# A two-block transformer kernel on one core: new step table and token-tile projections in the second mixer

## The chip, the cores and the metric

One core of one Trainium2 chip runs the whole program. The metric is the device time of one execution in microseconds (us), the median over runs: 1990.09 us before (three runs, 1989.8 to 1990.51). A difference below 0.2% (4 us) can't be told from none.

## The reference, cut to what matters

256 tokens of width 1024 in float32 go through a first block of two layers (feed forward, attention mixer, feed forward) and a second block of two layers. The change touches only the mixer of the second block:

```python
z = rms_norm(x, ln_mix) @ w_in          # split into nsa q,k,v..., gla q,k,v,r,low, mem q, merge
o_nsa = nsa_attention(...)              # compressed + selected + window attention
o_gla = gated_linear_attention(...)     # rms_norm(o, norm_g) * silu(r)
o_mem = memory_attention(...)
gates = sigmoid(merge + b_merge)        # three of width 1024
merged = (gates[:, :, 0] * (o_nsa @ w_branch[0])
          + gates[:, :, 1] * (o_gla @ w_branch[1])
          + gates[:, :, 2] * (o_mem @ w_branch[2]))
x = x + merged @ w_out
```

## The kernel before, in words

**The stream of weights.** All weights of the projections arrive as 616 pieces of 128x1024 float32 (512 KB), in the order of use. SP (the DMA queue) loads a piece into `raw`, ACT rounds it into `hi` (L1270), POOL subtracts the two into `lo` (L542), in place of `raw`; in the mixers POOL does it in four quarters. There are 7 places for `raw`/`lo` and 5 for `hi`, so ACT can round piece c only after TensorE is done with piece c-5. TensorE multiplies each piece as hi·hi, hi·lo and lo·hi (L569, L570, L571): 12 matmuls of 512 columns for each piece, for two token tiles (m = 0 and 1) of 128 tokens. `round_piece` stands in ACT's program four pieces ahead of its use.

**The order of the mixer.** `mix2_work` is a table written by hand: behind each of the four pieces of a strip (512 columns of `w_in`) or of a branch projection ("rows") it lists the small steps to do there. `mix2_order` makes one list of it, and TensorE (PE), ACT and VectorE (DVE) each walk through that list in order and do their own part of every step, so a step's place in it is its place on all three engines. Waits between engines are semaphores; each engine runs strictly in its order. A "take" (PSUM to SBUF, by ACT or DVE) stands behind the fourth piece of each strip, ahead of that piece's steps.

**The steps.** `mem_unit` t (mu): scores of unit t, transposes of t-1 (L750), outputs of t-2. `nsa` 0 to 6: the compressed keys, a chain of small operations between PE and DVE. `nsa_unit` t (nu): t = 0 is the compressed attention (PE L1077, DVE L2211 to L2231, ACT L1610 between them); odd t makes the scores (PE L773) of two units; every t > 1 transposes unit t-1 (L750, which waits for DVE's normalised probabilities, L1858, and for bank `turned`, freed by DVE's copy L1866); even t from 4 on also makes outputs (L760). `gla` 2: log-sigmoid on ACT and two scans on DVE (L2082, L2084). `decay` hp,i: i = 0 and 1 subtract on DVE (L2112), then ACT makes Abs and Exp (L1591, L1592), i = 2 and 3 multiply on DVE (L2121, L2122). `gla_unit` hp,t (gu): masked scores (PE L982 and, for t = 2, two extra matmuls L972 into `turned`; DVE L2148), for t = 2 and 4 first an output (PE L997) into `turned`, copied by DVE (L2133). `gla` 3 to 5 are the norm of the gated linear attention: squares on ACT (L1529), variance on DVE (L1726), the product with silu(r) (L2090), the root, the scaling (L2093); `gla` 6 and 7 transpose (L1032).

**The end of the mixer.** The branch projections come in the order 2 (memory), 0 (nsa), 1 (gla), four pieces each. Branch 2 and branch 0 use PSUM banks 0 to 3, two for each token tile; branch 1 uses 4 to 7. The strip ahead (`gr`, r of the linear attention) leaves in banks 0 and 1 by Silu on ACT (L1564), and an `exp_and_ln()` (preload of a table) follows it. The three gates' Sigmoids (L1627) stand behind the first three pieces of branch 2. DVE's `branch(b, m)` (L2266) multiplies gate and projection once all four pieces of the branch are through, for both token tiles; PE starts branch 0 when `branch` has counted both tiles of branch 2. After branch 1, `merged` is transposed and multiplied by `w_out`.

Of the kernel before, what the change touches and what calls it, by code (L numbers as in the profile page):

```python
# [15 lines left out]
ALU = mybir.AluOpType  # L16
# [3 lines left out]
P = 128  # L20
# [92 lines left out]

ROWS2 = {2: 0, 0: 0, 1: 4}


def mix2_work():

    windows, prep, mem, memory_in, gla, nsa = (
        [(name, i) for i in range(9)] for name in ("windows", "prep", "mem", "memory_in", "gla", "nsa"))  # L120
    cmp = [("cmp", k // 4, k % 4) for k in range(8)]
    mu = [("mem_unit", t) for t in range(6)]
    gu = [[("gla_unit", hp, t) for t in range(5)] for hp in range(2)]
    decay = [[("decay", hp, i) for i in range(4)] for hp in range(2)]
# [85 lines left out]
def tiles(a):  # L210
# [4 lines left out]

    "hi", "lo", "used", "quarter",

# [334 lines left out]
def pe_program(M, V, sem):  # L552
# [33 lines left out]

    def rows_tile(c, m, kt, a_hi, a_lo, bank, start, stop):

        slot, slot_hi = c % RING, c % RING_HI
        for i in range(2):  # L590
            w = slice(i * 512, i * 512 + 512)
            t = product(psum[:, bank + 2 * m + i, :], a_hi[:, kt, m * P:m * P + P], a_lo[:, kt, m * P:m * P + P],
                        hi[:, slot_hi, w], lo[:, slot, w], start, stop)
        return t

    def rows(c, kt, a_hi, a_lo, bank, start, stop=False, second=None):

        pe.wait_ge(sem["lo"], c + 1)
        for m in range(MT):
            if m and second:  # L600
                pe.wait_ge(sem[second[0]], second[1])
            t = rows_tile(c, m, kt, a_hi, a_lo, bank, start, stop)
        t.then_inc(sem["used"], 1)

    def half_rows(c, m, kt, a_hi, a_lo, bank, stop):

        if m == 0:
            pe.wait_ge(sem["lo"], c + 1)
        t = rows_tile(c, m, kt, a_hi, a_lo, bank, False, stop)
        if m:  # L610
            t.then_inc(sem["used"], 1)
        elif stop:
            t.then_inc(sem["f"], 1)

    def last_rows(c, kts, a_hi, a_lo, bank, turn, ylo={}):

        for m in range(MT):
            for i, kt in enumerate(kts):
                if m and i == len(kts) - 1 and turn:
                    turn()  # L620
                if m == 0 and i in ylo:
                    pe.wait_ge(sem["ylo"], ylo[i])
                half_rows(c + i, m, kt, a_hi, a_lo, bank, i == len(kts) - 1)

# [65 lines left out]
    def feed_forward(c, strips, gated, n0, turn_next):  # L690
# [20 lines left out]
        def down(c, s):  # L711
            pe.wait_ge(sem["ylo"], s + 1)
            for i in range(kts):
                rows(c + i, (s - n0) % 2 * kts + i, y_hi, y_lo, 4, s == n0 and i == 0)

# [14 lines left out]
        order = [(strips - s) % 2 * kts + i for s in ((2, 1) if gated else (1,)) for i in range(kts)]  # L730
        last_rows(c, order, y_hi, y_lo, 4, turn_next, {kts: n0 + strips} if gated else {})
        return c + 4
# [52 lines left out]
    def mix1(layer, c0, turn_next):  # L785
# [64 lines left out]
        for step in mix1_order():  # L850
# [48 lines left out]
            elif what == "rows":  # L899
                i, kt = step[1:]  # L900
                if i == 0:
                    pe.wait_ge(sem["z4"], layer + 1)
                pe.wait_ge(sem["y1lo"], 7 * layer + Y1_EVENT[kt])
                rows(c0 + 24 + i, kt, y_hi, y_lo, 0, i == 0, second=("z5", layer + 1) if i == 0 else None)
            elif what == "half":
                m, i = step[1:]
                kt = OUT_ORDER[-4:][i]
                pe.wait_ge(sem["y1lo"], 7 * layer + Y1_EVENT[kt])
                half_rows(c0 + 24 + KD - 4 + i, m, kt, y_hi, y_lo, 0, i == 3)
            elif what == "turn":  # L910
                turn_next()
# [4 lines left out]
    def mix2(layer, c0, turn_next):  # L916
# [39 lines left out]
        def gla_score(hp, u):  # L956
# [7 lines left out]
            if u == 2:  # L964
                wait_free("turned")
                order = [(0, None)] + order + [(1, None)]
            for hh, i in order:
                half = slice(64 * hh, 64 * hh + 64)
                if i is None:
                    if hh:  # L970
# [137 lines left out]
        for step in mix2_order():  # L1108
# [82 lines left out]
            elif what == "rows":  # L1191
                b, i = step[1:]
                if b == 2 and i == 0:
# [8 lines left out]
                pe.wait_ge(sem["y2lo"], 10 * layer + Y2_EVENT[kt])  # L1202
                rows(piece[step], kt, y_hi, y_lo, ROWS2[b], i == 0, i == 3)
            elif what == "last_branch":
# [6 lines left out]
                enter(V.merged, (0, 1, 2, 3), "merged", 4 * layer, c,  # L1211
                      lambda cc, m, j: rows_tile(cc, m, j, h_hi, h_lo, 4, j == 0, False), lambda j: j // 2)
                pe.wait_ge(sem["xlo"], 8 * n["feats"])
                last_rows(c + 4, range(4, KD), h_hi, h_lo, 4, turn_next)
                c += KD
# [23 lines left out]
def act_program(M, V, sem, landed):  # L1239
# [246 lines left out]
    def mix2(layer, c0, rstd):  # L1486
# [52 lines left out]
        for step in mix2_order():  # L1539
# [13 lines left out]
            elif what == "take":  # L1553
# [6 lines left out]
                elif name == "gr":  # L1560
# [5 lines left out]
                    t.then_inc(sem["z_gr"], 1)  # L1566
                    exp_and_ln()
            elif what == "prep" and step[1] == 0:
# [52 lines left out]
            elif what == "gate":  # L1621
# [68 lines left out]
def dve_program(M, V, sem):  # L1690
# [297 lines left out]
    def mix2(layer, c0, rstd):  # L1988
# [78 lines left out]
        def gla_step(i):  # L2067
# [61 lines left out]
        def gla_unit(hp, t):  # L2129
            if t in (2, 4):  # L2130
                m = t // 2 - 1
                dve.wait_ge(sem["go"], nxt("go"))
                dve.tensor_copy(V.gqk[:, m, S * hp:S * hp + S], psum[:, TURNED, S:2 * S]).then_inc(sem["og"], 1)  # L2133
            if t < 4:

# [125 lines left out]
        def branch(b, m):  # L2261

            g = V.merge[:, m, b * D:b * D + D]
            dve.wait_ge(sem["sigmoid"], 6 * layer + 2 * (2, 0, 1).index(b) + m + 1)
            bank = ROWS2[b] + 2 * m
            t = dve.tensor_tensor(g, g, flat(psum[:, bank:bank + 2, :]), ALU.mult)  # L2266
# [11 lines left out]
        for step in mix2_order():  # L2278
# [304 lines left out]
```

## Time and profile before

| | us |
|---|---|
| median of the runs | 1990.09 |
| the profiled execution's own time | 1993.09 |
| its span, first to last instruction | 1991.4 |
| PE busy (98%) | 1960.1 |
| POOL busy (80%) | 1594.6 |
| ACT busy (52%) | 1045.1 |
| DVE busy (36%) | 719.2 |

PE is the engine that matters: each us in which it isn't idle, or in which it runs at the full clock, is a us of the whole. The second block's mixers lie at about 1022 to 1310 us (layer 0) and 1510 to 1800 us (layer 1); layer 1's is the pattern of layer 0's, and all rows in order of time below are of layer 1. In a row of the timeline, "[0.97 <-ACT kT L1399]" means that the engine was idle for 0.97 us ahead of it and what ended that. Neighbouring operations of one engine overlap a little, so a row's time and the distance to the next row differ.

### The profile page before, as it was taken

The numbers are of one execution on the slowest core, as the hardware profiler recorded it, in microseconds if no ns is written. First come the engines' busy times: TensorE is split into PE (matmuls) and PEld (weight loads), VectorE is DVE, ScalarE is ACT, GpSimd is POOL, SyncE is SP. The second block draws the span as 40 slices with busy tenths as digits, with TensorE's granted clock in tenths as the row PEclk, the third lists the DMA queues.
The fourth block names the chain that finished last, engine by engine and source line by source line (L and its number), as shares of the span: only waits on it lengthen the run. The fifth ranks groups of instructions, "written<-read, shape, count | busy, mean of one in ns | idle before, by whom it ended". The sixth has DMA issues, their size and how long they took to land.

```text
span 1991.4 us, 26549 instructions
## 1 busy us (share of the span) xinstructions
PE 1960.1 (98%) x9698; PEld 1583.5 (80%) x9698; DVE 719.2 (36%) x1686; ACT 1045.1 (52%) x1748; POOL 1594.6 (80%) x1160
## 2 busy tenths in 40 slices
PE   9999999999999999999999999999999999999999
PEld 7888777888888877788887877788888777778887
DVE  3534444000300454410045667521115576642111
ACT  6445666444644566644475444654446554555443
POOL 7888776988788887698879577888888867788886
PEclk9999999999999999999999999999999999999999
DMA  6665434555665543556564333456657433335553
GB/s 234 234 207 178 153 125 153 186 190 187 214 212 188 173 165 117 169 188 247 190 253 159 108 119 124 147 173 228 204 178 264 138 128 117 125 133 196 182 186 131
DMA packets 98204, 348.63 MB, mean 175 GB/s; under 512 B 13436, under 2 KB 14108, under 8 KB 97820
## 3 DMA queue, kind: packets, MB, share of 16 engines
q1 hardware_dynamic: 97372, 345.80, 51.3%
q8 instruction: 78, 1.28, 0.3%
q10 hardware_dynamic: 704, 1.14, 0.2%
q14 instruction: 50, 0.41, 0.1%
HBM read 345.85 MB, written 1.05 MB: 174 GB/s over the span
## 4 chain that ended last, share of the span: by engine, by line
PE 95%; DVE 2%; POOL 1%; issue 1%; ACT 1%; DMA 0%; SPq 0%; DVEq 0%; ACTq 0%
PE psum L569 28%; PE psum L571 28%; PE psum L570 27%; PE psum L707 2%; PE psum L750 1%; PE psum L637 1%; PE psum L760 1%; POOL lo L542 1%; PE psum L982 1%; PE psum L773 1%; PE psum L740 1%; PE psum L1136 0%; PE psum L837 0%; PE psum L796 0%; DVE big L2112 0%
## 5 line engine op out<-in xcount | busy, mean ns | idle before, releaser
L542 POOL TENSOR_TENSOR lo<-raw,hi 128x256 fp32r<-128x256 f32 (+1 forms) x1156 | 1594.4, 1403 | 382.6 <-ACT hi L1270 354.9
L1270 ACT ACTIVATE hi<-raw 128x1024 fp32r<-128x1024 f32 x616 | 647.6, 1059 | 512.2 <-PE psum L571 485.7
L569 PE MATMUL psum<-hi,h_hi 128*128 128x512 f32 x1632 | 654.0, 401 | 1.9 <-POOL lo L542 1.4
L571 PE MATMUL psum<-hi,h_lo 128*128 128x512 f32 x1632 | 639.6, 392 | 0.0
L570 PE MATMUL psum<-lo,h_hi 128*128 128x512 f32 x1632 | 638.8, 391 | 0.0
L569 PEld LDWEIGHTS psum<-hi,h_hi 128*128 128x128 f32 x1632 | 308.5, 189 | 72.5 <-POOL lo L542 5.3
L571 PEld LDWEIGHTS psum<-hi,h_lo 128*128 128x128 f32 x1632 | 307.9, 189 | 66.4
L570 PEld LDWEIGHTS psum<-lo,h_hi 128*128 128x128 f32 x1632 | 308.3, 189 | 60.3
L569 PE MATMUL psum<-hi,y_hi 128*128 128x512 f32 x832 | 334.9, 402 | 4.9 <-DVE big L2266 4.9
L1811 DVE SCALAR_TENSOR_TENSOR big<-psum,small,big 128x256 f32<-128x256 f32 (+1 forms) x120 | 61.1, 550 | 749.5 <-ACT big L1363 749.5
L571 PE MATMUL psum<-hi,y_lo 128*128 128x512 f32 x832 | 326.2, 392 | 0.0
L570 PE MATMUL psum<-lo,y_hi 128*128 128x512 f32 x832 | 325.4, 391 | 0.0
L569 PEld LDWEIGHTS psum<-hi,y_hi 128*128 128x128 f32 x832 | 156.9, 189 | 40.0 <-DVE big L2266 5.7
L571 PEld LDWEIGHTS psum<-hi,y_lo 128*128 128x128 f32 x832 | 157.0, 189 | 34.2
L570 PEld LDWEIGHTS psum<-lo,y_hi 128*128 128x128 f32 x832 | 157.4, 189 | 30.3
L1412 ACT ACTIVATE soft<-soft,small 128x128 f32<-128x128 f32 (+1 forms) x120 | 54.6, 456 | 131.7 <-DVE small L1847 104.5
L1363 ACT ACTIVATE big<-psum,small 128x256 f32<-128x256 f32 (+1 forms) x120 | 57.2, 528 | 84.0 <-PE psum L571 84.0
L1819 DVE TENSOR_TENSOR y_lo<-psum,y_hi 128x512 fp32r<-128x512 f32 (+1 forms) x60 | 49.4, 823 | 38.3 <-ACT y_hi L1372 38.3
L1745 DVE SCALAR_TENSOR_TENSOR h_lo<-psum,special,h_hi 128x128 fp32r<-128x128 f32 x160 | 44.1, 343 | 42.5 <-ACT h_hi L1287 42.5
L1287 ACT ACTIVATE h_hi<-psum,special 128x128 fp32r<-128x128 f32 x160 | 44.6, 380 | 23.2 <-PE psum L637 23.2
L1372 ACT ACTIVATE y_hi<-psum 128x512 fp32r<-128x512 f32 (+1 forms) x60 | 42.8, 714 | 13.1 <-PE psum L707 13.1
L1866 DVE COPY soft<-psum 128x384 f32<-128x384 f32 (+2 forms) x68 | 35.4, 520 | 27.5 <-PE psum L750 27.5
(264 smaller groups left out, 1363.5 us busy)
## 6 DMA issues: line engine op xcount, KB each, us to landing
raw<-in_stream SPq DMA_DIRECT2D x616, 512.0 KB, 3.3
big<-in_w SPq DMA_DIRECT2D x14, 512.0 KB, 7.6
big<-in_post SPq DMA_DIRECT2D x6, 512.0 KB, 5.8
special<-in_b_merge SPq DMA_DIRECT2D x2, 1536.0 KB, 8.0
memkv<-in_mem SPq DMA_DIRECT2D x2, 1024.0 KB, 5.8
big<-in_band SPq DMA_DIRECT2D x2, 768.0 KB, 4.8
x<-in_x SPq DMA_DIRECT2D x2, 512.0 KB, 5.3
special<-in_special SPq DMA_DIRECT2D x2, 512.0 KB, 4.4
```

The source lines that it names most:

```text
L542: t = pool.tensor_tensor(M.lo[:, slot, w], M.raw[:, slot, w], f32(M.hi[:, slot_hi, w]), ALU.subtract)
L569: pe.matmul(out, lhs_hi, rhs_hi, start=start, stop=False)
L570: pe.matmul(out, lhs_hi, rhs_lo, start=False, stop=False)
L571: return pe.matmul(out, lhs_lo, rhs_hi, start=False, stop=stop)
L1270: act.activation(M.hi[:, slot_hi, :], M.raw[:, slot, :], ACT.Copy).then_inc(sem["hi"], 1)
L1287: t = act.activation(out_hi[:, k, toks], psum[:, bank, i * P:i * P + P], ACT.Copy, scale=1.0 if gain is None else gain[:, k:k + 1])
L1363: t = act.activation(act_s[:, m, :], psum[:, bank + m, 0:width], ACT.Silu if gated else ACT.Relu, scale=V.scale[:, m:m + 1])
L1372: act.activation(flat(out), flat(psum[:, bank:bank + kts // 2, :]), ACT.Copy).then_inc(sem["yhi"], 1)
L1412: t = act.activation(out, prob[:, w], ACT.Exp, scale=-1.0, bias=mn[:, i:i + 1], accum_out=total[:, i:i + 1])
L1745: t = dve.scalar_tensor_tensor(out_lo[:, k, toks], psum[:, bank, i * P:i * P + P], gain[:, k:k + 1], f32(out_hi[:, k, toks]), ALU.mult, AL ...
L1811: t = dve.scalar_tensor_tensor(prod_s[:, m, :], psum[:, bank + m, col:col + width], V.scale[:, m:m + 1], act_s[:, m, :], ALU.mult, ALU.mult)
L1819: dve.tensor_tensor(flat(y_lo[:, kt, :]), flat(psum[:, bank:bank + kts // 2, :]), f32(flat(y_hi[:, kt, :])), ALU.subtract).then_inc(sem["y ...
```

## The change

It moves steps in the table, gives branch 2 and branch 0 their PSUM banks by token tile, splits waits by token tile, and removes one of ACT's table preloads.

```diff
-ROWS2 = {2: 0, 0: 0, 1: 4}
+ROWS2 = {2: (2, 0), 0: (2, 0), 1: (4, 6)}          # banks of token tile 0, of token tile 1
...
-        "gqk": ([mu[1], nsa[0]], [mu[2]], [mu[3], nsa[1]], [nsa[6], nsa[2]]),
+        "gqk": ([mu[1]], [nsa[0], mu[2]], [mu[3], nsa[1]], [nsa[6], nsa[2]]),
         "gv": ([mu[4], nsa[3]], [gla[0]], [mu[5], nsa[4]], [gla[1], nsa[5]]),
-        ("merge", 0): ([nu[0], gla[2]], [decay[0][0]], [nu[1], decay[0][1]], [decay[0][2]]),
-        ("merge", 1): ([nu[2], decay[0][3]], [nu[3]], [gu[0][0]], [nu[4]]),
-        ("merge", 2): ([gu[0][1]], [nu[5]], [gu[0][2]], [nu[6]]),
+        ("merge", 0): ([gla[2], nu[0]], [decay[0][0]], [nu[1], decay[0][1]], none),
+        ("merge", 1): ([nu[2], decay[0][2]], [nu[3]], [decay[0][3]], [nu[4]]),
+        ("merge", 2): ([gu[0][0]], [nu[5]], [gu[0][1]], [nu[6], gu[0][2]]),
...
-        ("rows", 2): ([nu[17], gu[1][4]], [nu[18]], [gla[3]], [gla[4]]),
-        ("rows", 0): ([gla[5]], [gla[6]], [gla[7]], none),
+        ("rows", 2): ([nu[17]], [nu[18], gu[1][4]], [gla[3], gla[4]], [gla[5]]),
+        ("rows", 0): (none, [gla[6]], [gla[7]], none),
...
     def rows(c, kt, a_hi, a_lo, banks, start, stop=False, second=lambda: None):
         pe.wait_ge(sem["lo"], c + 1)
         for m in range(MT):
+            if m:
+                second()
             t = rows_tile(c, m, kt, a_hi, a_lo, banks, start, stop)
+            if stop and m == 0:
+                t.then_inc(sem["rows"], 1)
...
             if u == 2:                                   # gla_score
-                wait_free("turned")
-                order = [(0, None)] + order + [(1, None)]
+                order = order[:4] + [(0, None)] + order[4:] + [(1, None)]   # the wait now at (0, None)
...
                 if b == 2 and i == 0:                    # PE, rows
-                    evicted(len(names) + 1)
                     evicted(len(names))
+                    second = lambda: evicted(len(names) + 1)
                 if b == 0 and i == 0:
-                    pe.wait_ge(sem["branch"], 4 * layer + 2)
+                    pe.wait_ge(sem["branch"], 4 * layer + 1)
+                    second = lambda: pe.wait_ge(sem["branch"], 4 * layer + 2)
...
                     t.then_inc(sem["z_gr"], 1)           # ACT, behind the Silus of "gr"
-                    exp_and_ln()
...
                     act.activation(w, w, ACT.Sigmoid).then_inc(sem["sigmoid"], 1)
-            elif what == "branch":
-                if step[1:] == (2, 0):
+                if b == 1:                               # behind the last gate
                     exp_and_ln()
...
+            elif i == 3:                                 # DVE, gla_step
+                dve.wait_ge(sem["og"], n["og"])
+                dve.wait_ge(sem["z_gr"], layer + 1)
+                own(dve.tensor_tensor(r3, r3, f3, ALU.mult))
             elif i == 4:
                 dve.wait_ge(sem["ss"], nxt("ss"))
                 variance(V.cells8, P)
-                dve.wait_ge(sem["z_gr"], layer + 1)
-                own(dve.tensor_tensor(r3, r3, f3, ALU.mult))
...
                 b, m = step[1:]                          # DVE, branch
-                dve.wait_ge(sem["used"], piece["rows", b, 3] + 1)
+                if m:
+                    dve.wait_ge(sem["used"], piece["rows", b, 3] + 1)
+                else:
+                    dve.wait_ge(sem["rows"], nxt("rows"))
                 branch(b, m)
```

## Rows read from the trace of the kernel before

**Rows 1.** Page, busy time of each engine (us, share, instructions).
```profile
PE 1960.1 (98%) x9698; PEld 1583.5 (80%) x9698; DVE 719.2 (36%) x1686; ACT 1045.1 (52%) x1748; POOL 1594.6 (80%) x1160
```
**Rows 2.** Who PE waited for in layer 1's mixer: total us, times, longest.
```profile
PE psum L750 <- DVE soft L1858: 3.0, 2, 2.9
PE psum L569 <- DVE big L2266: 2.4, 1, 2.4
PE psum L972 <- DVE big L2133: 1.2, 2, 0.6
```
**Rows 3.** Table by windows: us, busy (x count) of PE, PEld, DVE, ACT, POOL; clock; DMA.
```profile
1096.00:1100.00 4.00, 4.00 (x11) 3.10 (x11) 3.08 (x7) 0.00 (x0) 2.99 (x5) 0.57 0.00 0
1540.00:1620.00 80.00, 77.66 (x427) 59.89 (x426) 45.66 (x104) 40.45 (x95) 66.00 (x88) 1.00 0.40 132
1642.00:1646.00 4.00, 4.00 (x14) 3.13 (x13) 4.00 (x8) 0.75 (x3) 3.86 (x4) 0.57 0.00 0
```
**Rows 4.** Timeline of PE and DVE around nsa[0]: start, us, operation, idle before.
```profile
1584.52 1.05 PE L1043 MATMUL psum<-consts,extra 128*128 128x32 f32 x8 [1.25 <-DVE soft L1866]
1594.12 0.60 PE L750 MATMUL psum<-consts,soft 128*128 128x128 f32 x4
...
1585.61 0.29 DVE L2162 COPY extra<-psum 128x128 f32<-128x128 f32 x1
1588.07 0.64 DVE L2166 TENSOR_SCALAR extra<-extra 128x128 f32<-128x128 f32 x1
1589.43 0.48 DVE L2055 TENSOR_SCALAR_CACHE_REDUCE soft<-psum,small 128x256 f32<-128x256 f32 x1 [0.72 <-PE psum L939]
```
**Rows 5.** Timeline of PE and DVE in merge strips 0 and 1.
```profile
1641.72 0.55 PE L750 MATMUL psum<-consts,soft 128*128 128x128 f32 x3 [2.88 <-DVE soft L1858]
...
1622.38 0.49 DVE L2211 TENSOR_TENSOR extra<-psum,consts 128x128 f32<-128x128 f32 x2 [2.62 <-PE psum L1077]
1626.31 0.68 DVE L2082 SCALAR_TENSOR_TENSOR big<-big,extra 128x512 f32<-128x512 f32 x1
1627.02 1.76 DVE L2084 TENSOR_TENSOR_SCAN extra<-consts,big 128x256 f32<-128x256 f32 x2
1638.35 1.21 DVE L2122 TENSOR_TENSOR big<-big,kT 128x1024 f32<-128x1024 f32 x1
1640.13 1.53 DVE L1858 TENSOR_SCALAR soft<-soft,small,extra 128x128 f32<-128x128 f32 x2
```
**Rows 6.** Table by windows, POOL's `lo` alone: us, busy of PE, PEld, POOL; clock, DMA.
```profile
1637.40:1647.05 9.65, 2.64 (x5) 1.08 (x4) 9.43 (x8) 0.82 0.16 54
1647.10:1662.05 14.95, 5.48 (x14) 2.80 (x15) 14.27 (x20) 1.00 0.44 142
```
**Rows 7.** Timeline of DVE and PE around nu[6] and gu[0][2].
```profile
1668.96 1.41 DVE L2308 SCALAR_TENSOR_TENSOR big<-psum,small,special 128x512 f32<-128x512 f32 x2 [1.37 <-PE psum L571]
1670.62 0.55 DVE L1866 COPY soft<-psum 128x384 f32<-128x384 f32 x1
1671.28 1.46 DVE L1858 TENSOR_SCALAR soft<-soft,small,extra 128x128 f32<-128x128 f32 x2
...
1664.45 0.34 PE L972 MATMUL psum<-memkv,big 64*128 64x128 f32 x1 [0.61 <-DVE big L2133]
```
**Rows 8.** Groups by line on ACT, 1735 to 1755 us: busy, mean ns.
```profile
L1627 ACT ACTIVATE big<-big 128x1024 f32<-128x1024 f32 x6 | 6.0, 1046 | 0.0
```
**Rows 9.** Timeline of ACT, DVE, PE and POOL at the end of the mixer.
```profile
1737.13 1.28 ACT L1259 ACT_TABLE_LOAD   x1
1751.49 1.04 ACT L1270 ACTIVATE hi<-raw 128x1024 fp32r<-128x1024 f32 x1
...
1751.67 2.35 DVE L2266 TENSOR_TENSOR big<-big,psum 128x1024 f32<-128x1024 f32 x2 [4.80 <-PE psum L571]
...
1754.08 0.50 PE L569 MATMUL psum<-hi,y_hi 128*128 128x512 f32 x1 [2.44 <-DVE big L2266]
1785.26 0.50 PE L569 MATMUL psum<-hi,h_hi 128*128 128x512 f32 x1 [0.44 <-POOL lo L542]
```

More of the change, by code:

```diff
@@ L214 @@
 SEMAPHORES = (
-    "hi", "lo", "used", "quarter",
+    "hi", "lo", "used", "rows", "quarter",
     "x_in0", "x_in1", "ident", "const", "rot", "pre1", "pre2", "par", "mem_in", "masks", "angles", "stored", "w1_0", "w1_1",
@@ L585, in strip_piece, with rows_tile @@
         t.then_inc(sem["used"], 1)
-    def rows_tile(c, m, kt, a_hi, a_lo, bank, start, stop):
+    def rows_tile(c, m, kt, a_hi, a_lo, banks, start, stop):
         slot, slot_hi = c % RING, c % RING_HI
@@ L591, in rows_tile, with rows, half_rows @@
             w = slice(i * 512, i * 512 + 512)
-            t = product(psum[:, bank + 2 * m + i, :], a_hi[:, kt, m * P:m * P + P], a_lo[:, kt, m * P:m * P + P],
+            t = product(psum[:, banks[m] + i, :], a_hi[:, kt, m * P:m * P + P], a_lo[:, kt, m * P:m * P + P],
                         hi[:, slot_hi, w], lo[:, slot, w], start, stop)
         return t
-    def rows(c, kt, a_hi, a_lo, bank, start, stop=False, second=None):
+    def rows(c, kt, a_hi, a_lo, banks, start, stop=False, second=lambda: None):
         pe.wait_ge(sem["lo"], c + 1)
         for m in range(MT):
-            if m and second:
-                pe.wait_ge(sem[second[0]], second[1])
-            t = rows_tile(c, m, kt, a_hi, a_lo, bank, start, stop)
+            if m:
+                second()
+            t = rows_tile(c, m, kt, a_hi, a_lo, banks, start, stop)
+            if stop and m == 0:
+                t.then_inc(sem["rows"], 1)
         t.then_inc(sem["used"], 1)
-    def half_rows(c, m, kt, a_hi, a_lo, bank, stop):
+    def half_rows(c, m, kt, a_hi, a_lo, banks, stop):
         if m == 0:
             pe.wait_ge(sem["lo"], c + 1)
-        t = rows_tile(c, m, kt, a_hi, a_lo, bank, False, stop)
+        t = rows_tile(c, m, kt, a_hi, a_lo, banks, False, stop)
         if m:
@@ L613, in half_rows, with last_rows @@
             t.then_inc(sem["f"], 1)
-    def last_rows(c, kts, a_hi, a_lo, bank, turn, ylo={}):
+    def last_rows(c, kts, a_hi, a_lo, banks, turn, ylo={}):
         for m in range(MT):
@@ L622, in last_rows @@
                     pe.wait_ge(sem["ylo"], ylo[i])
-                half_rows(c + i, m, kt, a_hi, a_lo, bank, i == len(kts) - 1)
+                half_rows(c + i, m, kt, a_hi, a_lo, banks, i == len(kts) - 1)
     def turned_tile(src, m, pairs, banks, ready, until):
@@ L713, in down @@
             for i in range(kts):
-                rows(c + i, (s - n0) % 2 * kts + i, y_hi, y_lo, 4, s == n0 and i == 0)
+                rows(c + i, (s - n0) % 2 * kts + i, y_hi, y_lo, (4, 6), s == n0 and i == 0)
         c += 4
@@ L730, in feed_forward @@
         order = [(strips - s) % 2 * kts + i for s in ((2, 1) if gated else (1,)) for i in range(kts)]
-        last_rows(c, order, y_hi, y_lo, 4, turn_next, {kts: n0 + strips} if gated else {})
+        last_rows(c, order, y_hi, y_lo, (4, 6), turn_next, {kts: n0 + strips} if gated else {})
         return c + 4
@@ L903, in mix1 @@
                 pe.wait_ge(sem["y1lo"], 7 * layer + Y1_EVENT[kt])
-                rows(c0 + 24 + i, kt, y_hi, y_lo, 0, i == 0, second=("z5", layer + 1) if i == 0 else None)
+                rows(c0 + 24 + i, kt, y_hi, y_lo, (0, 2), i == 0, second=lambda: pe.wait_ge(sem["z5"], layer + 1))
             elif what == "half":
@@ L908, in mix1 @@
                 pe.wait_ge(sem["y1lo"], 7 * layer + Y1_EVENT[kt])
-                half_rows(c0 + 24 + KD - 4 + i, m, kt, y_hi, y_lo, 0, i == 3)
+                half_rows(c0 + 24 + KD - 4 + i, m, kt, y_hi, y_lo, (0, 2), i == 3)
             elif what == "turn":
@@ L969, in gla_score @@
                 if i is None:
-                    if hh:
+                    if not hh:
+                        wait_free("turned")
+                    else:
                         pe.wait_ge(sem["rowtile"], nxt("rowtile"))
@@ L1192, in mix2 @@
                 b, i = step[1:]
+                second = lambda: None
                 if b == 2 and i == 0:
-                    evicted(len(names) + 1)
                     evicted(len(names))
+                    second = lambda: evicted(len(names) + 1)
                 if b == 0 and i == 0:
-                    pe.wait_ge(sem["branch"], 4 * layer + 2)
+                    pe.wait_ge(sem["branch"], 4 * layer + 1)
+                    second = lambda: pe.wait_ge(sem["branch"], 4 * layer + 2)
                 if b == 1 and i == 0:
@@ L1202, in mix2 @@
                 pe.wait_ge(sem["y2lo"], 10 * layer + Y2_EVENT[kt])
-                rows(piece[step], kt, y_hi, y_lo, ROWS2[b], i == 0, i == 3)
+                rows(piece[step], kt, y_hi, y_lo, ROWS2[b], i == 0, i == 3, second)
             elif what == "last_branch":
@@ L1211, in mix2 @@
                 enter(V.merged, (0, 1, 2, 3), "merged", 4 * layer, c,
-                      lambda cc, m, j: rows_tile(cc, m, j, h_hi, h_lo, 4, j == 0, False), lambda j: j // 2)
+                      lambda cc, m, j: rows_tile(cc, m, j, h_hi, h_lo, (4, 6), j == 0, False), lambda j: j // 2)
                 pe.wait_ge(sem["xlo"], 8 * n["feats"])
-                last_rows(c + 4, range(4, KD), h_hi, h_lo, 4, turn_next)
+                last_rows(c + 4, range(4, KD), h_hi, h_lo, (4, 6), turn_next)
                 c += KD
@@ L2133, in gla_unit @@
                 dve.tensor_copy(V.gqk[:, m, S * hp:S * hp + S], psum[:, TURNED, S:2 * S]).then_inc(sem["og"], 1)
+                n["og"] += 1
             if t < 4:
@@ L2264, in branch @@
             dve.wait_ge(sem["sigmoid"], 6 * layer + 2 * (2, 0, 1).index(b) + m + 1)
-            bank = ROWS2[b] + 2 * m
+            bank = ROWS2[b][m]
             t = dve.tensor_tensor(g, g, flat(psum[:, bank:bank + 2, :]), ALU.mult)
@@ L2336, in mix2 @@
                 b, m = step[1:]
-                dve.wait_ge(sem["used"], piece["rows", b, 3] + 1)
+                if m:
+                    dve.wait_ge(sem["used"], piece["rows", b, 3] + 1)
+                else:
+                    dve.wait_ge(sem["rows"], nxt("rows"))
                 branch(b, m)
```

## The prediction, made before the changed kernel ran

> **What bounds the kernel now.** I read the page's table of busy times first: PE is busy for 1960.1 of 1991.4 us [rows 1], so the whole is PE's work plus some 31 us in which it is idle or starts late. PE's matmuls stay as many and as large. The change can therefore only act through PE's idle time inside the two second-block mixers, and through what that idle time does to the clock. The second view was PE's list of waits over layer 1's mixer: 3.0 us for the probabilities (two waits, the longest 2.9), 2.4 for DVE's branch product, 1.2 for bank `turned` behind `gla_unit` [rows 2], and 1.25 ahead of nsa[0] [rows 4]. Layer 0 has the same waits to 0.1 us. The third view was the table by windows: in the 4 us behind the longest wait the granted clock is 0.57, that is, most of them ran at 1.2 GHz instead of 2.4. At 0.57, 4 x 0.43 = 1.7 us of PE time are lost. The 1.25 us wait has such a stretch behind it in layer 0 (1096 to 1100 us, 0.57) but not in layer 1 (clock 1.00 over 1540 to 1620 us) [rows 3]. So a wait over 2 us costs itself and 1.7 us more, one of 1.25 us sometimes does. The sums below are in us for one layer, on the profiled execution (1993.1 us, span 1991.4), and doubled at the end.
>
> **1. nsa[0] one piece later.** PE's 1.25 wait goes [rows 4]: the copy it waited for has a whole piece (2.7 us) to end. What is late next is DVE. Its nsa[0] chain of five operations (first at 1585.61, last ends at 1588.71: 3.1 us) ran beside a piece; now it stands ahead of mu[2]'s minimum, which started at 1589.43. PE would reach nsa[0]'s matmuls at about 1586.0 and end them at 1586.9; the chain then ends at 1590.1, 0.65 later than the minimum started before, and the probabilities behind it are ready at about 1593.4. PE arrives at their transpose (L750, 1594.12 before) 1.25 earlier, at 1592.9, and waits some 0.6. Net gain 0.6 (bounds 0 and 1.25). In layer 0 the low clock behind the old wait should go too: 1.7, once.
>
> **2. The probabilities of nsa unit 2's transpose.** PE waited 2.88 at 1641.72 for L1858, which ended at 1641.66 [rows 5]. Two things leave DVE's queue ahead of it. The linear attention's rest (L2082 0.68 and the scans, 2.5 together) ran behind nu[0]; now it goes ahead of it, into DVE's 2.62 of idle time before L2211. It waits for ACT's three operations there, which I put at 1618.8 to 1620.8, so it ends at 1623.4 and nu[0] starts 1.0 later: 1.5 of 2.5 is saved. And the first decay multiplication (L2121 and L2122, alike, 1.21 each with overlap, 2.3 together) moves behind that L1858. Together 3.8: ready at 1637.9, against PE's arrival at 1641.72 - 2.88 = 1638.8, or 1638.7 without the smaller wait of 0.17 of the same group [rows 2]. The cover is 0.8. I take the whole 2.88 + 0.17 + 1.7 for the clock = 4.75. Bounds: 2.05 (1 us of wait comes back and the clock falls all the same) and 4.75. What is late next: the last decay multiplication, needed at gu[0][0], which now stands one piece later; by the same count DVE ends it near 1646, PE comes near 1649.
>
> **3. gu[0][2] right behind nu[6].** Before, a piece lay between. Now PE transposes (L750), and its next matmul writes the same bank, so it waits for DVE's copy L1866, which stands behind the take of merge strip 2: L2308 starts when the piece ends (1668.96), L1866 ends at 1671.17, and PE is through with L750 at about 1670.05. A wait of 1.1. Then DVE still has L1858 (1.46, to 1672.74) ahead of the copy L2133 that frees the bank again. PE's output matmuls end near 1672.0, four of the scores (0.07 each) hide 0.3, and it waits some 0.9 more. New waits 2.0, against 0.61 before [rows 7]: a loss of 1.4. Behind PE are the scores of that unit and piece 0 of merge strip 3; nobody else is late for them. Bounds: a loss of 0.5 (L1858 takes about 0.7 where POOL is idle) and of 3.1 (the clock falls as well). For the clock I charge one fall over both layers.
>
> **4. Four scores ahead of the wait in `gla_score`.** For gu[1][2] the wait of 0.61 [rows 2] loses the time of four matmuls: gain 0.3 (0 to 0.6).
>
> **5. The end of the mixer.** The table load behind Silu goes (1.28), and `gr`'s and branch 2's banks no longer tie PE to ACT; PE wasn't waiting there. The load of Sigmoid's table stays, since it follows Silu's directly, and the load for Exp and Ln moves ahead of the squares. ACT's line from Silu's end at 1737.13 is full in both versions: three roundings, six Sigmoids of 1.0 [rows 8], two loads, a high part, the squares of 2.35, which ended before 1751.49 [rows 9]. By the same durations it comes to 1751.3. DVE now takes the variance of these squares *before* `branch(2, 0)`, so the branch product, free to start at 1749.3 by the new semaphore, starts at about 1751.45 (before: 1751.67). PE, which saves the 0.74 wait and gets here at 1750.7, needs only the first of the two products (2.35 / 2): it starts branch 0 near 1752.8 instead of 1754.08, still after 2 us of idle and so with the low clock. Gain 1.2. The second product ends at 1754.0, under PE's six matmuls at either clock. Behind it POOL is the next to be late: PE already waited 0.44 for `lo` at 1785.26 [rows 9], and pieces there come back to back. I keep 1.0. Bounds: 0.4, and 4.1 if wait and clock both go. L2090 (1.8) moves from the branch to a place where DVE was idle; nothing hangs on it.
>
> The rest (DVE's `branch(0, 0)` half a piece earlier, `z_gr` for one tile only) lies beside PE's work: nothing.
>
> **Sum.** 0.6 + 4.75 - 1.4 + 0.3 + 1.0 = 5.25 in each layer, 10.5 for two; plus 1.7 for layer 0's clock in step 1, less 1.7 for one fall in step 3: 10.5. The profiled execution would take 1982.6, and the median 1990.1 - 10.5 = **1979.6 us**.
>
> **A rule that speaks against it.** POOL's pieces took 9.43 / 2 = 4.7 us over 1637 to 1647, beside DVE's multiplications, and 14.27 / 5 = 2.9 over 1647 to 1662 [rows 6]. The Trainium skill (SBUF — State Buffer, section "SBUF: two separate sides") says that a DVE operation with two SBUF inputs and a GpSimd operation exclude each other for a whole instruction; the trace agrees as far as these numbers go. It would make a denser DVE queue a slower POOL, which is the last rival below.
>
> **Rivals.**
> - *Half of it comes back (0.18).* Step 2's cover of 0.8 is less than one operation, and step 3's two waits may both lower the clock. Then step 2 gives 2.9 (1 us of wait back in both layers, the low clock in one: 3.75 and 2.05) and step 3 costs 3.1: 0.6 + 2.9 - 3.1 + 0.3 + 1.0 = 1.7, with layer 0's 1.7 a gain of 5.1: 1985.0. For it: L1858 took 1.46 and 1.53 in two places. Against: each of these needs two waits to be longer than I count.
> - *The end's wait goes whole (0.12).* If ACT is 1.5 us earlier at the squares than I add up, PE meets no wait over 1 us and no low clock: 3.1 more in each layer, 1973.4. For it: the product itself could start at 1749.3. Against: ACT's line has no gap to lose.
> - *The waits are only exchanged (0.08).* DVE is the late engine from 1622 to 1647 without a pause; if the postponed multiplications make PE wait at gu[0][0] as long as it waited before, step 2 gives nothing: 0.5 in each layer and 1.7, 1987.4 or up to no change.
> - *POOL takes over, and it is slower (0.06).* Place: merge strips 0 to 3, 16 pieces, where PE takes about 4.0 a piece with the steps between. If the denser DVE keeps POOL at 4.7 for all of them, POOL falls behind by 0.7 x 16 = 11 less the 5 us of lead it has there, 6 us of waits, and with every such wait the clock (two falls, 3.4): 9.4 - 5.25 = 4 lost in each layer, about 1997. It decides once POOL's mean piece there passes 4.3; it was 3.5 (24.6 us for seven) in [rows 6].
>
> **How the numbers follow.** Forecast 0.56, 1979.6. Its own range is 1976 to 1983. For 8 in 10, I reach to the first rival above and partly to the second below: 1975 to 1986.5. A measurement of this kernel tells about 0.2%, 4 us, from no change. Faster by more: 0.56 + 0.12 + 0.15 of the first rival = 0.83. Within: 0.03 + 0.08 = 0.11. Slower: 0.06.
>
> **What would show it.** Step 1: no wait of L1043, one of about 0.6 at an L750 some 9 us later, clock 1.00 near 1096. Step 2: no wait over 1 us for L1858, clock 1.00 around 1640. Step 3: two new waits in nu[6] and gu[0][2], for L1866 and L2133, 1.1 and 0.9. Step 5: a wait of some 2 us for L2266 remains, DVE's product starts right behind the variance, and each of the two mixers has one table load less. Wrong would be: a wait for `lo` that grows past 2 us in a layer, the L1858 wait still there, or a gain below 5 us in all.

## The result and the profile after

The changed kernel takes **1975.14 us** (median of 4 runs, 1974.72 to 1976.92), the kernel before 1990.3 beside it (1989.8 to 1991.71): a ratio of 0.9918 [0.9907, 0.993]. It is faster, by more than forecast: 1979.6 was predicted, with 1976 to 1983 as the forecast's own range, so the time lies 0.9 below its lower end. The profiled execution took 1974.96 us (span 1972.9), against 1993.09 (1991.4): 18.5 us of span to explain, where the steps had given 10.5.

Page of the changed kernel: span, then busy times as in [rows 1].
```profile
span 1972.9 us, 26543 instructions
PE 1951.8 (99%) x9698; PEld 1578.3 (80%) x9698; DVE 719.3 (36%) x1686; ACT 1041.4 (53%) x1746; POOL 1592.1 (81%) x1160
```
PE has the same 9698 matmuls in 8.3 us less of busy time, though none was removed: most of that is the clock (four falls fewer, below, at 1.7 each: 6.8). The other 10 us are idle time that is gone. ACT has two instructions less, one table load in each of the two mixers.

Who PE waited for in layer 1's mixer of the changed kernel, as in [rows 2]: total us, times, longest.
```profile
PE psum L569 <- DVE big L2272: 2.0, 1, 2.0
PE psum L1000 <- DVE soft L1869: 1.2, 1, 1.2
PE psum L742 <- ACT kT L1404: 1.0, 1, 1.0
PE psum L569 <- POOL lo L542: 0.7, 2, 0.4
```
(The changed kernel has new line numbers, and in the kernels of the experiments they differ by one more or less: L2272 is the branch product that was L2266, L1869 the copy L1866, L1861 the probabilities L1858, L2138 the copy L2133; L752, L1000 and L975 were L750, L997 and L972.) The 2.9 for the probabilities, the two of 0.6 for L2133 and the 1.25 ahead of nsa[0] [rows 2, 4] are gone. L742's 1.0 was there before. One wait is new: 1.2 at L1000.

Table by windows of the changed kernel, as in [rows 3]: one of the times at which the clock had fallen before, nearly all of the time from layer 0's mixer to the branch wait of layer 1 (1040 to 1735), and the 4 us at that wait.
```profile
1096.00:1100.00 4.00, 4.00 (x27) 3.59 (x27) 3.56 (x10) 0.75 (x3) 2.01 (x3) 1.00 0.38 131
1040.00:1735.00 695.00, 684.86 (x3691) 545.64 (x3689) 347.85 (x834) 369.02 (x684) 559.28 (x568) 1.00 0.46 162
1735.00:1739.00 4.00, 3.35 (x8) 2.68 (x9) 3.86 (x7) 1.37 (x4) 3.67 (x6) 0.59 0.31 118
```
Before, the clock fell five times in the two mixers (behind both L1858 waits, both branch waits and one of the two 1.25 waits). Now it falls once, behind the branch wait of layer 1.

Timeline of the changed kernel around nsa[0], as in [rows 4].
```profile
1575.05 0.97 PE L1046 MATMUL psum<-consts,extra 128*128 128x32 f32 x8
1581.80 0.66 PE L752 MATMUL psum<-consts,soft 128*128 128x128 f32 x4
...
1576.06 0.29 DVE L2168 COPY extra<-psum 128x128 f32<-128x128 f32 x1 [1.28 <-PE psum L1046]
1578.14 0.23 DVE L2172 TENSOR_SCALAR extra<-extra 128x128 f32<-128x128 f32 x1
1578.40 0.48 DVE L2058 TENSOR_SCALAR_CACHE_REDUCE soft<-psum,small 128x256 f32<-128x256 f32 x1
...
1572.59 5.11 POOL L542 TENSOR_TENSOR lo<-raw,hi 128x256 fp32r<-128x256 f32 x7
1581.32 2.79 POOL L542 TENSOR_TENSOR lo<-raw,hi 128x256 fp32r<-128x256 f32 x4 [3.62 <-ACT hi L1275]
```
DVE's chain of five took 2.3 us (1576.06 to 1578.37), not the 3.1 of [rows 4], and PE went through L752 without a wait. POOL was idle from 1577.70: its next piece wasn't rounded yet. The last two operations of the chain, which started after that, took 0.29 and 0.23; beside POOL's piece they had taken 0.73 and 0.64.

Timeline of the changed kernel around gu[0][2], as in [rows 7].
```profile
1651.26 0.68 PE L1000 MATMUL psum<-big 128*128 128x128 f32 x4 [1.17 <-DVE soft L1869]
1651.87 0.72 PE L985 MATMUL psum<-memkv,big 64*128 64x128 f32 x8
1652.46 0.37 PE L975 MATMUL psum<-memkv,big 64*128 64x128 f32 x1
...
1651.22 0.67 DVE L1861 TENSOR_SCALAR soft<-soft,small,extra 128x128 f32<-128x128 f32 x2
1651.97 0.42 DVE L2138 COPY big<-psum 128x256 f32<-128x256 f32 x1
```
The wait of 1.1 for the copy is there as forecast (1.17). The second, of 0.9 for L2138, is not: L1861 took 0.67 us instead of 1.46, although POOL was at work beside it (one row of `lo`, 1646.36 to 1655.43), and the four scores ahead of the wait (eight matmuls of the trace, 1651.87 to 1652.46) cover the copy that ends at 1652.39.

Timeline of the changed kernel at the end of the mixer, as in [rows 9].
```profile
1730.42 1.28 ACT L1264 ACT_TABLE_LOAD   x1
1734.07 1.04 ACT L1275 ACTIVATE hi<-raw 128x1024 fp32r<-128x1024 f32 x1
...
1734.27 0.17 DVE L1729 TENSOR_SCALAR small<-small 128x8 f32<-128x8 f32 x1 [3.86 <-ACT big L1534]
1734.38 2.35 DVE L2272 TENSOR_TENSOR big<-big,psum 128x1024 f32<-128x1024 f32 x2
...
1735.65 0.73 PE L569 MATMUL psum<-hi,y_hi 128*128 128x512 f32 x1 [2.01 <-DVE big L2272]
```
This is step 5 as written: the product starts right behind the variance, PE after the first half of it, still after 2 us of idle.

**Stage by stage** (profiled executions, differences of the starts of the same PE instructions): the span ahead of the first mixer gave 1.0 us, which is no edit's (the start of one and the same PE instruction there lies between 1037.5 and 1039.1 us in the profiles of all kernels); layer 0's mixer 9.7; layer 1's 7.7; the end 0.1.

### The profile page after: what moved, and what is told of

Same layout as the page of the kernel before. It is cut to its first block, busy times and chain, and to the rows that moved or that the text cites. A ratio compares the mean times of both kernels' runs of the same rounds, so it can differ in the third digit from the quotient of the medians.

```text
span 1972.9 us, 26543 instructions
## 1 busy us (share of the span) xinstructions
PE 1951.8 (99%) x9698; PEld 1578.3 (80%) x9698; DVE 719.3 (36%) x1686; ACT 1041.4 (53%) x1746; POOL 1592.1 (81%) x1160
## 4 chain that ended last, share of the span: by engine, by line
PE 94%; POOL 2%; ACT 2%; DVE 1%; issue 0%; DMA 0%; SPq 0%; POOLq 0%; ACTq 0%; DVEq 0%
PE psum L569 28%; PE psum L571 27%; PE psum L570 27%; POOL lo L542 2%; PE psum L709 2%; PE psum L752 1%; PE psum L639 1%; PE psum L775 1%; PE psum L762 1%; PE psum L985 1%; PE psum L742 1%; ACT big L1631 1%; ACT hi L1275 0%; PE psum L1139 0%; PE psum L798 0%; PE psum L839 0%
## 5 line engine op out<-in xcount | busy, mean ns | idle before, releaser
L1869 DVE COPY soft<-psum 128x384 f32<-128x384 f32 (+2 forms) x68 | 35.4, 520 | 24.9 <-PE psum L752 24.9
```

## The experiments

Each kernel ran four or five times (the one of 5: 11 times) beside the kernel before, which took 1992.3 to 1993.1 us (medians of 9, 9, 15 and 9 runs) in these four sessions; the changed kernel, run again in two of them, took 1975.4 and 1975.71. Differences below are from 1975.5. The part ahead of the mixers, which no edit touches, varied by 1.6 us between the profiles, so a difference of 1 or 2 us between two medians carries little. "A fall" is a short stretch in which TensorE's granted clock drops from 2.4 to 1.2 GHz, as behind the waits of [rows 3]; PE loses 1.7 us in it. Experiments are called by their numbers.

**1. The middle alone** (the kernel before with the table's new rows for merge strips 0 to 2).
```diff
-        ("merge", 0): ([nu[0], gla[2]], [decay[0][0]], [nu[1], decay[0][1]], [decay[0][2]]),
+        ("merge", 0): ([gla[2], nu[0]], [decay[0][0]], [nu[1], decay[0][1]], none),
...                                                   # and the rows of strips 1 and 2
```


> The kernel before with the new merge rows of the table alone (linear attention's rest ahead of nu[0], decay multiplications later, gu[0][2] right behind nu[6]). Theory A, waits as the trace of the changed kernel has them and 1.7 us for each stretch of low clock: the L1858 wait goes with its clock (4.75 in each layer), gu[0][2] costs one wait of 1.17, nothing for the second: 3.6 in each layer, 1983. Theory B, the sizes of my forecast (two new waits, 1.4, and one fall of the clock): 2.5 in each layer, 1985.3.

1984.31 us (1982.52 to 1985.34), ratio 0.9959 [0.9946, 0.9971].
Its waits in layer 1:
```profile
PE psum L569 <- DVE big L2266: 2.4, 1, 2.4
PE psum L997 <- DVE soft L1866: 1.9, 2, 1.2
PE psum L569 <- POOL lo L542: 1.4, 2, 1.2
PE psum L1043 <- DVE soft L1866: 1.3, 1, 1.3
PE psum L972 <- DVE big L2133: 1.2, 2, 0.6
```
The L1858 wait and the clock fall behind it are gone in both layers; of the 2.0 us of new waits that I had added for gu[0][2], 1.2 came (L997), and the 0.6 at L972 is the old one. Half of the whole gain is these three rows. The other half, 8.8 us, is for the most part waits listed here: per layer 1.25, 1.2 (L972), 0.74 (the second L997) and 0.43 of the branch wait, 3.6 x 2 = 7.2. The 1.6 left would be the size of one fall, but that is not shown: the profile, of the fastest of its runs, has one in the mixers, at layer 0's branch wait, as many as the changed kernel's.

**2. nsa[0] back in its place** (the changed kernel with `"gqk": ([mu[1], nsa[0]], [mu[2]],` again).

> The changed kernel with nsa[0] back at its old place. Theory A: the 1.25 us wait is back in both layers, and the clock falls behind about one of the two: 2.5 + 1.7 = 4.2 slower than the changed kernel, 1979.3. Theory B, my forecast's net gain of 0.6 in each layer and 1.7 once: 2.9 slower, 1978.0. If such a wait never lowers the clock: 2.5 slower and as many low-clock stretches as in the changed kernel.

1979.4 us (1978.75 to 1980.5), ratio 0.9935 [0.9921, 0.9948]: 3.9 slower than the changed kernel. The wait of 1.25 is back in both layers (2.5), and the profile has a fall at 1095.6 us behind layer 0's. Step 1 is worth 1.25 a layer, and 1.6 where the clock fell. (In layer 1, without a fall, PE's stretch over nsa[0] is 1.5 us longer than in the changed kernel, so here the wait cost a little more than its idle time.)

**3. The end back** (banks, semaphores, rows and the preload as before; the table of the middle and the order of the scores changed).

> The changed kernel with the old end of the mixer (banks, waits, table loads, gla[3] to gla[5] and gu[1][4] at their old places). Theory A: waits of 2.44 and 0.74 against 2.01, and POOL's waits for lo smaller in return; the low clock behind both 2.44 waits against one of two now: 1 us in each layer and 1.7 once, 3.5 slower than the changed kernel, 1978.6. Theory B, my forecast: 2 slower, 1977.

1978.45 us (1977.69 to 1979.36), ratio 0.993 [0.9917, 0.9942]: 3.0 slower. The waits of 0.74 and 2.44 (against 2.01) are back, 1.17 a layer; the rest of the 3.0 isn't placed.

**4. The order of the scores back** (the wait for `turned` ahead of all scores again).
```diff
-                order = order[:4] + [(0, None)] + order[4:] + [(1, None)]
+                wait_free("turned")
+                order = [(0, None)] + order + [(1, None)]
```


> The changed kernel with the wait for bank turned ahead of all of gla_score's matmuls again. Waits as in the kernel before, about 0.6 at gu[0][2] and gu[1][2] in each layer: 4 x 0.6 = 2.4 slower than the changed kernel, 1977.6. My forecast had 0.3 for each: 1.2 slower, 1976.4. No low clock from them in either.

1979.98 us (1978.01 to 1980.79), ratio 0.9937 [0.9925, 0.995]: 4.5 slower, where I had given step 4 0.3 a layer. Around gu[0][2] in that kernel:
```profile
1653.88 0.68 PE L999 MATMUL psum<-big 128*128 128x128 f32 x4 [1.17 <-DVE soft L1868]
1655.17 0.34 PE L974 MATMUL psum<-memkv,big 64*128 64x128 f32 x1 [0.61 <-DVE big L2137]
```
0.61 is back at both gated units of each layer (gu[0][2] and gu[1][2]): 2.4 us in all. The scores moved ahead of the wait are worth 0.61 twice a layer, not 0.3 once. That leaves 2 us; the profile is of the fastest of the five runs and has no fall in the mixers, so falls in the others are possible, but not shown.

**5. gla[2] ahead of nu[0] alone** (the kernel before with `[gla[2], nu[0]]`): which half of step 2 does it?

> The kernel before with gla[2] ahead of nu[0] alone; the decay multiplications stay. My sum for step 2 has two parts, 1.5 us from this and 2.3 from the multiplications: the wait for L1858 falls from 2.88 to 1.4 in both layers, 3.0 less, and the clock falls behind it once instead of twice: 4.7 faster than the kernel before (1992.3 in the runs so far), 1987.6. If either part alone is enough, the wait is gone: 9.2 faster, 1983.

1990.06 us (1986.83 to 1990.46, 11 runs), ratio 0.9986 [0.9977, 0.9994]: less than either expectation. PE in merge strip 1 of layer 1:
```profile
1639.56 0.55 PE L750 MATMUL psum<-consts,soft 128*128 128x128 f32 x3 [1.89 <-DVE soft L1858]
1644.52 1.16 PE L982 MATMUL psum<-memkv,big 64*128 64x128 f32 x16 [1.66 <-DVE small L1847]
```
The 2.88 [rows 5] becomes 1.89: this half is worth 1.0 and not the 1.5 of the forecast. PE runs into DVE again 4 us later (1.66), where the decay multiplications still stand ahead. The waits grow by 0.7 a layer; what the kernel gains is the fall, which in its profile comes behind neither. The table's postponed multiplications (`decay[0][2]` and `[0][3]` behind nu[2] and nu[3]) are the other half of step 2. With both, in experiment 1, L1858 ends 0.6 us before PE comes (1631.55 against 1632.12), so this half is worth some 2.5 (1.89 + 0.6), an estimate for 2.3 forecast. The multiplications moved without gla[2] were not tried.

**6. The remaining wait at branch 0.** Can its 2.0 us go? First with only the variance behind the branch products (`[gla[3]], [gla[4], gla[5]]`), then with the squares behind them too, with and without gla[6] and gla[7] a piece later:

> The changed kernel with gla[4] (the variance, which waits for ACT's squares) moved behind the fourth piece of branch 2, that is behind DVE's branch products. Theory C, DVE's order is what PE waits for: the wait of 2.0 for L2272 goes in both layers, with the low clock where it fell: 4.0 + 1.7 = 5.7 faster than the changed kernel, 1969.5. Theory D, POOL is the bound through the end of the mixer (its pieces from branch 0's last to the fourth of w_out come back to back, 31.5 us for nine): the wait for L2272 goes, and one for lo of about 3 us comes at the fourth piece of w_out, with a low clock behind it: 0 to 1.5 faster, 1973.6 to 1975.1.

> The changed kernel with gla[3] to gla[5] behind branch 2's fourth piece, but gla[6] and gla[7] left where the change has them (in e7 they were one piece later, and PE waited 4.3 us for the bank that DVE's L2104 frees behind four branch operations). Theory D: no wait at branch 0 (2.0 before), POOL's line starts 2.3 us earlier, so none over 0.5 for lo either, at most 0.3 at L1035: 3 us in each layer and the low clock of about one wait less, 1967.5 to 1970. If the line of ACT and POOL still ends the mixer, as in e4: 1973 to 1975.

> The changed kernel with gla[3] to gla[5] all behind branch 2's fourth piece, and gla[6] and gla[7] one piece later, so that ACT rounds piece 539 ahead of the squares (2.3 us earlier) and DVE makes the branch products ahead of the variance. Theory D: both PE's wait for the product (2.0 with half a low-clock stretch) and POOL's start move by 2.3: 2.4 faster in each layer, 1970.3. If POOL's line doesn't start with ACT's rounding of 539: as e4, no gain, 1975. Rival: the scaled output of the linear attention comes too late, PE waits at L1035 or for DVE's L2104 behind four branch operations: 1973 to 1977.

1975.4 (1974.66 to 1975.86; 0.9914 [0.99, 0.9927]), 1975.84 (1975.33 to 1976.54; 0.9918 [0.9904, 0.9931]) and 1982.46 us (1980.93 to 1983.15; 0.9951 [0.9937, 0.9965]). In the first two the branch wait is gone from both layers, and nothing is gained. Waits of the second one in layer 1:
```profile
PE psum L569 <- POOL lo L542: 2.2, 2, 2.0
```
Its POOL, from branch 0 on; PE waits until 1763.87:
```profile
1733.36 3.81 POOL L542 TENSOR_TENSOR lo<-raw,hi 128x256 fp32r<-128x256 f32 x4 [1.44 <-ACT hi L1275]
1738.71 30.40 POOL L542 TENSOR_TENSOR lo<-raw,hi 128x256 fp32r<-128x256 f32 x33 [1.54 <-ACT hi L1275]
```
33 operations (eight pieces in quarters and one whole) without a gap over 0.15 us; the piece that PE waits for is the seventh, which ends at 1763.82. So from 1738.71 POOL sets the pace. In the third kernel gla[7]'s copy, which frees a bank that PE needs, stands behind the four DVE operations of the branches, and PE waits 4.30 us for it (`<-DVE y_lo L2104`), with a fall in each layer.

**7. Making that wait longer.** PE to wait for both branch products (`pe.wait_ge(sem["branch"], 4 * layer + 2)` ahead of token tile 0), and the third table load back behind Silu:

> The changed kernel, but PE waits for both branch products before branch 0's first piece, as the kernel before did. Theory D: the wait grows by one product, 2.0 to 3.2, and PE's waits for lo behind it (0.43; 0.42 and 1.30) shrink in return: 0 to 0.8 in each layer, and a low clock more often: 1976 to 1978.5. Theory of the forecast, the split as a plain gain of 1.2 in each layer: 1977.5 plus the clock.

> The changed kernel with the table load behind Silu put back (1.28 us of ACT). Theory D: ACT's line from Silu to the squares has no gap, so squares, PE's wait at branch 0 (2.0 to 3.3) and POOL's line behind them all move by 1.28: 2.6 slower for two layers, and 1.7 more where the clock falls behind the longer wait: 1977.7 to 1979.4. If ACT's line has room: no change.

1978.37 (1977.41 to 1980.31; 0.9931 [0.9918, 0.9943]) and 1978.7 us (1978.01 to 1979.29; 0.9933 [0.9921, 0.9946]): 2.9 and 3.2 slower. The wait is 3.15 and 3.44 in both layers (1.1 and 1.4 more), with a fall behind each. So the split by token tile and the removed load are each worth a little over 1 us of wait a layer, and something more where a longer wait brings a fall.

**8. POOL's line relieved.** POOL takes some of the last pieces of a mixer whole instead of in quarters (`return 8 <= at < 64` in `in_mixer`: 12 whole; 72: 4; 70: 6), in the changed kernel (12, 4) and in the second kernel of 6 (4, 6).

> The changed kernel with POOL's subtraction in one operation instead of four quarters from branch 0's first piece to the end of the mixer. A whole piece took 2.40 us against 3.1 to 3.9 in quarters. Theory D (POOL's line of pieces 539 to 547 is the bound behind ACT): the waits for lo at the fourth piece of w_out (0.43 and 1.30) go, and no others: 1.7 faster than the changed kernel, 1973.4. Rival: DVE's operations with two SBUF inputs stand behind a whole piece and not a quarter, L2092 and L2098 end 1 to 2 us later and PE waits for L2104 or the branch products: 0 to 3 slower.

> The changed kernel with the last four pieces of each second mixer that POOL took in quarters (72 to 75) taken whole. A quarter-wise piece took POOL 2.9 us alone and 3.7 to 3.9 beside DVE, a whole one 2.4, so POOL's line gains some 3 us ahead of the first strip of the next stage. Theory: POOL's line ends the mixer wherever no clock fall slows PE there, so the waits of 1.30 and 0.25 for lo go in layer 0: 1.3 to 1.6 us less, 1973.5 to 1974.5, if DVE is not held for longer than PE's slack. Rival: DVE's last additions (L2278, L2282) are held by the whole pieces as in the kernel with twelve whole pieces, and PE waits 0.7 to 1.0 us for them in each layer: 1975 to 1977, no gain.

> As the kernel before, but with the variance and its root behind the branch products as well (gla[3] to gla[5] late). That kernel alone had no wait at branch 0 but 1.98 and 0.83 us (layer 0) and 2.01 us with a clock fall (layer 1) for lo, and 1975.8. Theory that POOL's line is what took the gain back: with 3 us off that line these waits go, and 1975.8 - 2.8 - 2.0 - 1.7 (the fall) = 1969.3, 1969 to 1971.5 with small waits left. Rival: DVE, held by whole pieces, is late instead: PE waits 1 to 2.4 us at L639 or for h_lo in each layer, 1973 to 1976.

> As the kernel before with six whole pieces (70 to 75) instead of four. Theory: POOL's line is already free of waits with four, so nothing more is gained, and DVE's branch additions L2278 beside pieces 70 and 71 are held: within 0.7 us of the kernel with four, or up to 1.5 above. Rival: four were too few, and this one is 1 to 2 us faster.

1980.97 (1980.77 to 1986.29; 0.9955 [0.9942, 0.9967]), 1977.13 (1976.56 to 1979.2; 0.9923 [0.9909, 0.9936]), 1977.06 (1976.56 to 1977.39; 0.9922 [0.9909, 0.9934]) and 1975.84 us (1975.47 to 1976.33; 0.9916 [0.9902, 0.9929]). Against 1975.5 that is 5.5, 1.6, 1.6 and 0.3 us slower. For 12 and for 4 the rival's mechanism held, and it cost more than the rivals' ranges said: a whole piece takes 2.4 us where four quarters took 2.8 to 3.9, the waits for `lo` shrink to 0.3 and less, and DVE is late in POOL's place. Six whole pieces came out 1.2 faster than four, as the rival there had it; if that is more than noise, why is open. DVE in the kernel with 12:
```profile
1740.49 0.97 DVE L1720 TENSOR_TENSOR small<-small 128x8 f32<-128x8 f32 x1
1741.49 2.32 DVE L1721 TENSOR_TENSOR small<-small 128x8 f32<-128x8 f32 x1
1743.85 2.34 DVE L1722 TENSOR_SCALAR small<-small 128x8 f32<-128x8 f32 x1
1746.22 0.17 DVE L1723 TENSOR_TENSOR small<-small 128x8 f32<-128x8 f32 x1
```
The second and the third of these in the third kernel of 6, in a pause of POOL (1741.87 to 1743.41):
```profile
1742.62 0.17 DVE L1721 TENSOR_TENSOR small<-small 128x8 f32<-128x8 f32 x1
1742.83 0.17 DVE L1722 TENSOR_SCALAR small<-small 128x8 f32<-128x8 f32 x1
```
PE's waits of the kernel with 12:
```profile
PE psum L1035 <- DVE big L2098: 2.4, 1, 2.4
PE psum L569 <- DVE big L2272: 2.0, 1, 2.0
PE psum L1000 <- DVE soft L1869: 1.2, 1, 1.2
PE psum L639 <- DVE big L2282: 1.0, 2, 0.7
```
and waits of the third kernel, products first with four whole:
```profile
PE psum L639 <- DVE big L2282: 4.2, 4, 2.0
```
Operations on 128x8 that take 0.17 us elsewhere take 2.3 here, the length of one whole POOL piece. The Trainium skill (SBUF — State Buffer, section "SBUF: two separate sides") says that a DVE operation with two SBUF inputs and a GpSimd operation that reads SBUF hold a shared pair of ports for a whole instruction, and the other blocks; these rows agree (L1721, which has two inputs, took 2.32 beside pieces of 2.40; L1722, with one, was held too). So quarters don't make POOL fast: they bound what DVE can lose to one of them.

**9. The changed kernel again**, for comparison in two sessions.

> The changed kernel itself once more, as the measure for the runs beside it: 1975.1, within 1 us, from the waits of 1.17, 0.97 and 2.0 in each layer, with one or two stretches of low clock in an execution.

> The changed kernel itself, on the same chip as the three before, so that differences under 2 us can be read: 1974.7 to 1976.9, with one or two clock falls beside the one at the start.

1975.4 (1974.43 to 1976.71; 0.9917 [0.9903, 0.993]) and 1975.71 us (1975.51 to 1976.51; 0.9916 [0.9902, 0.9929]). No version beat it by more than the noise.

## Why the prediction was wrong

The direction and the mechanisms of steps 1, 2 and 5 were right. The gain was too small by 8.0 us of span, and all the edits' errors lie on one side. Terms of the sum in us, L0 and L1 for the layers, the last column with the number of the experiment:

| | forecast | measured | shown by |
|---|---|---|---|
| start, no edit | 0 | 1.0 | profiles |
| step 1, wait | 0.6 x 2 | 1.25 x 2 | 2 |
| step 1, clock L0 | 1.7 | 1.6 | 2 |
| step 2, wait and clock | 4.75 x 2 | 4.75 x 2 | 1, 5 |
| step 3, waits | -1.4 x 2 | -1.17 x 2 | 1 |
| step 3, clock | -1.7 | 0 | after, 1 |
| step 4 | 0.3 x 2 | 1.22 x 2 | 4 |
| step 5, wait | 1.0 x 2 | 1.17 x 2 | 3 |
| step 5, clock | 0 | 0.65 L0, 0.04 L1 | windows below |
| not placed | | 0.8 | |
| sum | 10.5 | 18.5 | |

- **Step 1**, "the chain then ends at 1590.1", failed by the duration: I moved a chain of 3.1 us as it stood, but part of its length came from POOL's piece beside it. At its new place POOL has a pause, the chain takes 2.3, and there is no new wait, though by little: the probabilities are ready 0.1 us before PE comes. Experiment 2 confirms the size of the whole step.
- **Step 2** held to its size, with its halves at 1.0 and some 2.5 (experiment 5) for 1.5 and 2.3.
- **Step 3 and step 4** were counted apart. I charged step 3 the second wait, 0.9 against 0.61 before, with L1858 at 1.46. It took 0.67, as in my own lower bound, but not for the reason given there, "where POOL is idle": POOL was at work beside it, and why it took 0.67 is open. And step 4's "time of four matmuls" misread the trace: it lists each of a unit's eight scores as two matmuls (16 rows of L985), so the four ahead of the wait are eight of 0.07, 0.59 us (1651.87 to 1652.46), and I counted them at one of the two gated units of a layer. Experiment 4 shows 0.61 with the old order and nothing with the new, at both. Told in the forecast's own terms, step 3 cost 0.56 a layer (1.17 less the old 0.61) and not 1.4, and step 4 gave 0.61 and not 0.3. That is the largest error of the waits, 2.3 us for two layers.
- **The fall charged for step 3** never came: behind waits of 1.2 us or less the clock held in every profile.
- **Step 5** went as forecast: wait 2.01 of 2.44, 0.74 gone.

At branch 0 a fall costs less than elsewhere. Windows from PE's start of branch 0 to the same later instruction, the kernel before in both layers, then the changed one (us, busy of PE, PEld, DVE, ACT, POOL; clock; DMA):
```profile
1266.06:1309.14 43.08, 42.17 (x187) 33.92 (x187) 21.18 (x27) 17.84 (x33) 38.86 (x39) 0.96 0.45 149
1754.08:1797.15 43.07, 42.17 (x187) 33.92 (x187) 21.17 (x27) 17.84 (x33) 38.85 (x39) 0.96 0.43 149
```
```profile
1255.97:1298.40 42.43, 40.47 (x186) 32.67 (x186) 21.14 (x26) 17.56 (x31) 38.83 (x41) 1.00 0.46 155
1735.65:1778.68 43.03, 42.15 (x187) 33.90 (x187) 20.44 (x26) 17.45 (x31) 38.89 (x41) 0.96 0.44 152
```
With a fall PE is busy 1.7 longer, but the stretch takes only 0.6 longer, because PE otherwise waits for POOL (1.30 at the same place of layer 0, 0.43 with the fall). POOL is busy for 38.8 us in each. The prediction named POOL as "the next to be late" and cut step 5 to 1.0; the kernels of 6 show that it is the limit: the last 2 us of the branch wait are worth nothing as long as POOL's line stays. Those of 8 show that whole pieces don't shorten that line for nothing.

**The base was off too.** I took the change off the median of three runs, 1990.09, and the steps' sizes from one execution of 1993.09 with five falls. In the later sessions the kernel before ran at 1992.3 to 1993.1 and the changed one at 1975.4 to 1975.7: 17 us apart. Single executions of before lay between 1989.7 and 1993.8. At 1.7 a fall that would be two or three falls more or less. From its own execution of 1993.09 the forecast gave 1982.6, against 1974.96. The lower base hid part of the error: the time missed by 4.5 us, the gain by 8.0, and that was luck.

**The rivals.** "The end's wait goes whole" needed ACT earlier than it was; the branch wait stayed (and 6 shows that its end alone would have given nothing). "Half of it comes back" and "exchanged" fell with the wait for L1861, of which nothing came back. "POOL takes over, slower" had the place wrong: in merge strips 0 to 3 PE never waited for `lo`; POOL binds later, at the pieces of `w_out` (1764 us in the kernels of 6).

## What to carry to other kernels

A step that is moved doesn't keep its duration: read what the neighbour engine does at the new place, for DVE above all whether POOL is at work there. Count the rows of an operation before you price it: here a float32 score was two of them. Price a clock fall by place: 1.6 to 1.7 us where PE alone sets the end, 0.6 at branch 0, where POOL's line ends just behind it. And before removing a wait, look whether the next engine in line has slack: here 2.0 us of PE idle could be removed at branch 0 and came back whole 28 us later.

## What the runs showed of the hardware

The same wait is followed by a clock fall in some executions and not in others. Over the 18 profiles, idle stretches of PE in the second block's mixers: of 2.8 to 4.3 us, a fall at 8 of 8; of 1.9 to 2.5 us, at 12 of 33; of 1.6 and 1.7, at none of 3; of 1.2 to 1.5, at 4 of 18; of 0.9 to 1.2, at none of 72. So no prediction of a single fall near 2 us is safe here. What decides stays open.
